# Constant products in the waits of the routing, and the weight products ahead of the first transposes

## The reference

```python
g_prob = jax.nn.softmax(x32 @ rg_w + rg_b, axis=-1)
g_val, g_idx = lax.top_k(g_prob, 1)
e_logits = (x32 @ re_w + re_b).reshape(t_tok, N_GROUPS, EXP_PER_GROUP)
sel = jnp.take_along_axis(e_logits, g_idx[:, :, None], axis=1)[:, 0]
e_val, e_idx = lax.top_k(sel, TOP_K)
weights = jax.nn.softmax(e_val, axis=-1) * g_val
...
xs = x[buf_tok].reshape(n_blocks, MOE_BLOCK, d)
h = jax.nn.silu(xb @ w1[e]) * (xb @ w3[e])
return h @ w2[e]
...
out = jnp.zeros((t_tok, d), jnp.float32).at[buf_tok].add(ys)
```

## Time and profile before

| what | us |
|---|---|
| median of 3 runs | 2529.59 |
| lowest and highest run | 2528.16, 2534.01 |
| profiled execution | 2537.29 |
| its span, on which the rows stand | 2535.6 |
| TensorE busy in the span | 2359.7 (93%) |
| VectorE, ScalarE, GpSimd busy | 1369.4, 1118.1, 673.4 |

### The profile page before, as it was taken

The page is one execution under the profiler, slowest core; times in us unless marked ns, Lnnn a source line. Parts: engine busy times, 40 slices in busy tenths (PEclk is TensorE's granted clock), DMA queues, the critical chain, the costliest instruction groups (busy, mean ns, idle before and its releaser), DMA issues. The chain is left out here.

```text
span 2535.6 us, 33774 instructions
## 1 busy us (share of the span) xinstructions
PE 2359.7 (93%) x11388; PEld 1854.2 (73%) x11389; DVE 1369.4 (54%) x1967; ACT 1118.1 (44%) x1444; POOL 673.4 (27%) x514
## 2 busy tenths in 40 slices
PE   6979899799999999999999999499999999999991
PEld 5757777688888888888888887377667766677771
DVE  6888575634444444434443444655555556547565
ACT  4523333133333333333333332457666666567673
POOL 3821101100000000000000000077555756567771
PEclk9989999899999999999999999699999999999996
DMA  7864747343354435543463333379777978799987
GB/s 238 321 233 156 240 169 238 89 147 94 106 195 141 125 94 169 179 125 94 119 222 94 100 96 112 141 251 339 276 256 270 340 263 270 261 328 346 328 296 285
DMA packets 311869, 516.31 MB, mean 204 GB/s; under 512 B 33180, under 2 KB 211616, under 8 KB 295392
## 3 DMA queue, kind: packets, MB, share of 16 engines
q1 hardware_dynamic: 295312, 458.17, 51.4%
q0 software_dynamic: 16464, 56.90, 8.9%
HBM read 430.33 MB, written 84.68 MB: 203 GB/s over the span
## 5 line engine op out<-in xcount | busy, mean ns | idle before, releaser
L1496 PE MATMUL mrgps<-xn_hi,w_hi 128*128 128x512 f32 x1024 | 401.4, 392 | 6.7 <-DVE w_lo L1615 6.7
L1496 PE MATMUL mrgps<-xn_hi,w_lo 128*128 128x512 f32 x1024 | 399.5, 390 | 0.0
L1496 PE MATMUL mrgps<-xn_lo,w_hi 128*128 128x512 f32 x1024 | 399.5, 390 | 0.0
L1998 POOL TENSOR_TENSOR w_lo<-w_raw,w_hi 128x1024 fp32r<-128x1024 f32 x128 | 343.0, 2836 | 0.0
L2159 PE MATMUL exps<-w_hi,x_room 128*128 128x512 f32 x1024 | 330.4, 399 | 4.9 <-issue 4.3
L1427 ACT ACTIVATE gt<-mrgps,mb 128x512 f32<-128x512 f32 x128 | 88.3, 690 | 509.1 <-PE mrgps L1496 503.0
L1761 POOL MEMSET x_ident<- 128x128 f32 x1 | 0.2, 205 | 1109.1 <-POOLq L1223 1109.1
L1993 DVE TENSOR_TENSOR w_lo<-w_raw,w_hi 128x2048 fp32r<-128x2048 f32 x126 | 283.5, 2310 | 0.0
L1632 DVE SCALAR_TENSOR_TENSOR tmp<-gt,mrgps 128x512 f32<-128x512 f32 x96 | 66.0, 688 | 387.0 <-PE mrgps L1496 387.0
L1983 ACT ACTIVATE w_hi<-w_raw 128x2048 fp32r<-128x2048 f32 x128 | 239.1, 1921 | 8.4 <-DMA w_raw<-in_expert_w_dram 8.3
L2159 PEld LDWEIGHTS exps<-w_hi,x_room 128*128 128x128 f32 x1024 | 193.2, 189 | 65.1 <-issue 18.3
(11 more groups left out here) (427 smaller groups left out, 4114.5 us busy)
## 6 DMA issues: line engine op xcount, KB each, us to landing
w_raw<-in_expert_w_dram SPq DMA_DIRECT2D x192, 1024.0 KB, 10.1
w_raw<-in_merge_gate_w_dram SPq DMA_DIRECT2D x128, 512.0 KB, 4.0
win_hi<-w_in_parts SPq DMA_DIRECT2D x42, 512.0 KB, 3.6
win_lo<-w_in_parts SPq DMA_DIRECT2D x42, 512.0 KB, 4.9
w_raw<-in_branch_w_dram SPq DMA_DIRECT2D x128, 128.0 KB, 4.1
wout<-in_w_out_dram SPq DMA_DIRECT2D x64, 256.0 KB, 4.5
w_raw<-in_x_dram SPq DMA_DIRECT2D x16, 512.0 KB, 9.7
branch_rows<-in_x_dram SPq DMA_DIRECT2D x16, 512.0 KB, 5.8
```

Source lines behind the costliest of these rows:

```text
L1496: last = pe.matmul(bank[:], w[:, u % 2, kk], x, start=(kk == w_tiles[0] and j == 0), stop=(kk == w_tiles[-1] and j == 2))
L1998: eng.tensor_tensor(self.lo2[:, f], self.raw2[:, f], self.hi2[:, f].bitcast(F32), ALU.subtract).then_inc(self.split2, 1)
```

## The change

TensorE gets a helper that multiplies `ones` by `below` into a new bank, `idle_ps`, which nothing reads. It is called three times: 30 products after the wait for the constants and ahead of the wait for `hot`, 44 after the two wide products, and 20 at the end of the stage. The eight transposes move from between the two halves of the weight products to behind both, with their waits for the identity and the gathered rows. The other engines' programs are the same; the bank of `first_x` moves up by one.

```diff
-        rank_ps, tot_ps, tab_ps, scale_ps, *first_x = (ctx.enter_context(nc.psum_tensor(f"rtps{i}", [P, 512], F32)) for i in range(6))
+        rank_ps, tot_ps, tab_ps, scale_ps, idle_ps, *first_x = (ctx.enter_context(nc.psum_tensor(f"rtps{i}", [P, 512], F32)) for i in range(7))
...
+            def keep_clock(n):
+                for _ in range(n):
+                    pe.matmul(idle_ps[:, 0:P], ones[:], below[:], start=True, stop=True)
+
             pe.wait_ge(consts, 10)
+            keep_clock(30)
             pe.wait_ge(hot_ready, 1)
             pe.matmul(tot_ps[:], ones[:], hot.rearrange("p t e -> p e t"), start=True, stop=True).then_inc(ranks, 1)
             pe.matmul(rank_ps[:], below[:], hot.rearrange("p t e -> p (t e)"), start=True, stop=True).then_inc(ranks, 1)
+            keep_clock(44)
...
             for k in range(2):
-                if k == 1:
-                    pe.wait_ge(wt.idn, 1)
-                    pe.wait_ge(wt.gathered, 16)
-                    for h in range(2):
-                        for q in range(4):
-                            last = pe.transpose(first_x[h][:, q * P:(q + 1) * P], wt.xg[:].rearrange("p (c k) -> p k c", k=KD)[:, 4 * h + q], wt.ident[:])
-                        last.then_inc(turned0, 1)
                 pe.wait_ge(scales_ready, k + 1)
                 for i in range(TT):
                     last = pe.matmul(scale_ps[:, 0:NBT], V[:, i, k].bitcast(F32), S[:, i, k], start=(i + k == 0), stop=(i == TT - 1 and k == 1))
             last.then_inc(scales_ps, 1)
+            pe.wait_ge(wt.idn, 1)
+            pe.wait_ge(wt.gathered, 16)
+            for h in range(2):
+                for q in range(4):
+                    last = pe.transpose(first_x[h][:, q * P:(q + 1) * P], wt.xg[:].rearrange("p (c k) -> p k c", k=KD)[:, 4 * h + q], wt.ident[:])
+                last.then_inc(turned0, 1)
+            keep_clock(20)
```

## The result

The changed kernel takes 2535.73 us (median of 17 runs, 2531.91 to 2541.71), the kernel before, on the same chip, 2531.87 us (median of 17, 2528.02 to 2536.43). The ratio is 1.0015, with a 95% interval of 1.0008 to 1.0022: slower by 3.9 us, 2.0 to 5.6 by the interval. The interval does not hold 1, and the ratio lies within the 0.2% that the prediction called the same. The 2535.73 us is over the 2534.7 that the prediction gave as its bound, but the kernel before came out 2.3 us higher in these runs too (2529.59 then), and the verdict goes by the ratio. The profiled execution has a span of 2534.5 us.

A forecast was written before the change was run, and what follows sets the result against it. TensorE ends the span; in the routing it waits on other engines at a halved clock. Terms -0.5 + 0 + 1.3 + 1.8 = +2.6 us on the 2529.59 us median gave 2532.2 us, range 2526.5 to 2537.0.

The forecast's parts named there:

- the two costs: End of the routing stage: weight products ahead of the transposes, +1.3 us, and 20 constant products before the drain, +1.8 us.
- the first term: 30 constant products before the wait for the picks: two wide products at 2.4 GHz, -0.5 us (bounds 0 and 1.0 earlier).
- The order: Both halves of the weight products ahead of the transposes: transposes start 2.7 us later, VectorE's drain ends later, +1.3 us.
- The last call: 20 constant products after the transposes: the drain waits for them, so the barrier opens later, +1.8 us.
- Rival (c): End of stage: the drain does not wait for the fillers, or products run in another order; +0.8 us, 2530.4 us, chance 0.07.
- The wide products: Two products after the picks: if the clock is kept they run at 2.4 GHz, 0.95 us earlier; half taken, -0.5 us.
- The table products: 44 constant products ahead of them: clock falls again before the second burst, so 0 (bounds -1.6 and 0).
- The start of the experts: First expert products behind the barrier: again at 1.2 GHz; possible loss and earlier clock rise in weight products set off, 0.
- Rival (a): Whole routing stage: fillers keep the clock up to the end and experts start at 2.4 GHz; -1.7 us, 2527.9 us, chance 0.13.
- Rival (b): Constant products in front run late at a low clock and delay real ones; +15.3 us, 2544.9 us; chance 0.12, a third in full.

## Why the prediction came out as it did

The forecast was 2.6 us over before, near where it came out: 3.9 us by the timed runs (2.0 to 5.6), 2.8 to 2.9 in the stage. Of the 3.5 us between the forecast of 2532.2 and the measured 2535.73, 2.3 are the kernel before, which came out that much higher, and 1.3 are the change. The mechanism of the two costs was right. That the sum came so near owes something to luck: the first term gave 0.4 us less than forecast, and the order cost 0.2 us less inside the changed kernel.

- **The order, +1.3 us**: right. 1.28 us by itself. In the changed kernel VectorE's drain ended 40.06 us after wide instead of 39.05, only 1.0 us later: 0.07 us came from the wide products, and the clock rose half a us earlier in the weight products than with the order alone (32.1 us after wide instead of 32.6).
- **The last call, +1.8 us**: right. In the changed kernel TensorE's drain ended 1.9 us after VectorE's, and the slope is 0.23 us for each product. Rival (c), a drain that does not wait, is refuted by two runs.
- **The wide products, -0.5 us**: wrong in size and in its reason. I took the price at the full clock from another float32 product of 512 columns, which reads in a row; this one reads with a step. The term came out at -0.07 us with the clock at 1.00 for the first 1.4 us: 2.05 us to VectorE's release instead of 2.12. The two wide products in the earlier trace rows gave no hint of it: at 0.50 a record takes some 0.9 us either way. The clock itself did what the term left open, held over the stall and lost 1.4 us into the wide products, and for this read it was worth nothing.
- **The table products, 0**: right in its result. The stall behind the 44 products was 3.8 us, within my 3.1 to 5.2, and the clock fell before the second burst, 4.4 us after the stop. (The clock's first rise came 2.9 us after the constant products began, a little ahead of my 3.3 to 6.2.)
- **The start of the experts, 0 on balance**: right in this profile (3.4 us at 0.50 in both). It is the term that varies: 6.8 us in the profile with the order alone, 1.0 us lost by it, and 6.8 us again with 40 products at the end.
- Rival (a), the clock kept to the end, is refuted for this kernel by its windows; with 108 constant products in front the clock still fell as the second burst began. Only with eight more between the bursts did one profile have the second burst at 1.00, and there the clock fell behind the wait for the gather. Rival (b) did not happen in the changed kernel, as every constant product in front ended in time, but it did, for 0.9 us, where eight stood between the bursts.

What stays open: the timed runs give 1 us more than the stage. Their interval covers the difference, and the profiles show no second place: from the first transposes of the first expert to the end the span has 856.7 us in both. Ahead of wide, where the kernels differ by nothing but constant products, the start of wide lies between 1615.6 and 1623.3 us in the 14 profiles, a spread of twice the effect of the change; behind the stage they have 855.7 to 857.4 us.

## What to carry to other kernels

Work that only keeps the clock up belongs where its engine would stand idle and nothing waits for its end. Ahead of a barrier it is paid one to one, since the drain waits for products that nobody reads; right behind the barrier, while registers load, three long ones gave back in the profile the 1.5 us that the slow start had cost. What a higher clock gains in front of a wait makes the wait longer: in the two profiles read for it TensorE then waited 2.4 and 2.6 us for the gather instead of 0.63, and lost the clock behind it. Before work is moved forward in a queue, ask what waits for the work behind it: here 16 products whose result is needed only for the last copy of the stage stood in front of the transposes that ScalarE and VectorE waited for, while the gathered rows were there.

## What I had not expected of the hardware

- A float32 product of 512 columns whose moving operand is read with a step of 128 bytes takes 0.86 us a record at the full clock and hardly more at the low one (1.87 us for two, against 1.80); in a row it takes 0.43 at the full one. Writing the bank with a step of 64 bytes cost nothing (1.02 us for the product, as for the next one, which writes in a row).
- The clock can fall when the engine is already at work again: 1.4 us into the wide products behind a stall of 3.36 us, 0.8 us into the table products behind one of 2.15 us, 0.2 us into the second burst behind one of 2.29 us. In the kernel before, the shortest stall behind which it fell was 2.55 us.
- 28 small records held TensorE's sequencer for 1.2 us, while they ran for 3.4.
